# VectorE instead of TensorE turns the layer input, with the retention output and the second memory layer's norm rearranged

## The reference, cut to what matters

```python
def first_block(x, mem, ...):
    for i in range(2):
        if i % 2 == 0:
            tok, mq, z = retention_branch(x, positions, w_in_ret[j], ret_norm_g[j])
        else:
            tok, mq, z = gdn_branch(x, w_in_gdn[j], ...)
        mem_out = memory_attention(mq, mem, w_mem_kv[i])   # kv = mem @ w_kv
        branch = concat([tok, mem_out]) * silu(z)
        y = branch @ w_out[i]
        x = layer_norm(ALPHA * x + y, ln_g[i], ln_b[i])
    return x
# retention, at its end, per head:
    mu, var = mean(o, -1), mean(square(o - mu), -1)
    o = (o - mu) * rsqrt(var + NORM_EPS) * norm_g
```

## Time and profile before

| | us |
|---|---|
| median of 3 runs | 2926.92 |
| lowest, highest | 2924.23, 2928.47 |
| the profiled execution, its time | 2937.41 |
| its span | 2935.6 |
| TensorE matmuls busy | 2867.0 (98%) |
| GpSimd busy | 2344.0 (80%) |
| ScalarE busy | 1364.8 (46%) |
| VectorE busy | 1205.2 (41%) |

### The profile page before, as it was taken

How to read it: one execution, slowest core, us unless ns; L and a number is a source line. 1 busy time by engine, 2 the same in 40 slices (tenths; PEclk the granted TensorE clock), 3 DMA queues, 4 the chain that set the end, 5 groups by cost and what they waited for, 6 DMA issues and landing times.

```text
span 2935.6 us, 40528 instructions
## 1 busy us (share of the span) xinstructions
PE 2867.0 (98%) x13819; PEld 2406.5 (82%) x13819; DVE 1205.2 (41%) x2325; ACT 1364.8 (46%) x1783; POOL 2344.0 (80%) x1831
## 2 busy tenths in 40 slices
PE   9989999999979999999999999999999999999998
PEld 7878788888868888888888888788887888888886
DVE  5253343434442433334333345486535332332334
ACT  4444444444434554544546354555435444444444
POOL 8978898888877665757667588788887999999997
PEclk9999999999999999999999999999999999999999
DMA  8545555555654444434444356444554655655553
GB/s 285 190 161 182 165 191 190 180 188 178 209 180 135 144 143 134 147 122 154 140 138 145 117 172 203 157 140 153 196 164 163 200 194 188 200 186 192 197 193 132
DMA packets 284353, 502.72 MB, mean 171 GB/s; under 512 B 18021, under 2 KB 68662, under 8 KB 283190
## 3 DMA queue, kind: packets, MB, share of 16 engines
q1 hardware_dynamic: 275606, 482.55, 50.0%
q10 hardware_dynamic: 8608, 18.24, 1.7%
HBM read 498.61 MB, written 2.12 MB: 171 GB/s over the span
## 4 chain that ended last, share of the span: by engine, by line
POOL 51%; issue 25%; PE 23%; POOLq 1%; DVE 0%; DVEq 0%; ACT 0%
POOL wlo L418 51%; PE acc L474 8%; PE acc L475 8%; PE acc L476 8%; POOLq L416 0%; POOLq L413 0%; DVE x_sb L2316 0%; POOLq L418 0%; DVE big L2292 0%; DVE kv L1808 0%; DVEq L154 0%; ACT small L1427 0%; DVE small L2283 0%; POOL eps_sb L412 0%; DVE small L2309 0%
## 5 line engine op out<-in xcount | busy, mean ns | idle before, releaser
L418 POOL TENSOR_TENSOR wlo<-raw,whi 128x512 fp32r<-128x512 f32 x1824 | 2343.5, 1317 | 574.5 <-ACT whi L1050 558.2
L1050 ACT ACTIVATE whi<-raw 128x1024 fp32r<-128x1024 f32 x910 | 957.5, 1060 | 1102.6 <-PE acc L476 1058.1
L474 PE MATMUL acc<-whi,a_lo 128*128 128x512 f32 x2528 | 1002.9, 397 | 37.5 <-DVE kv L1773 19.4
L476 PE MATMUL acc<-whi,a_hi 128*128 128x512 f32 x2528 | 988.7, 391 | 0.0
L475 PE MATMUL acc<-wlo,a_hi 128*128 128x512 f32 x2528 | 987.6, 391 | 0.0
L474 PEld LDWEIGHTS acc<-whi,a_lo 128*128 128x128 f32 x2528 | 477.4, 189 | 135.7 <-DVE kv L1773 19.9
L476 PEld LDWEIGHTS acc<-whi,a_hi 128*128 128x128 f32 x2528 | 476.5, 189 | 101.0
L475 PEld LDWEIGHTS acc<-wlo,a_hi 128*128 128x128 f32 x2528 | 477.4, 189 | 95.5
L474 PE MATMUL acc<-whi,b_lo 128*128 128x512 f32 x928 | 365.6, 394 | 0.0
L476 PE MATMUL acc<-whi,b_hi 128*128 128x512 f32 x928 | 361.4, 389 | 0.0
L475 PE MATMUL acc<-wlo,b_hi 128*128 128x512 f32 x928 | 361.2, 389 | 0.0
(11 more groups left out here) (291 smaller groups left out, 2103.2 us busy)
## 6 DMA issues: line engine op xcount, KB each, us to landing
raw<-in_w_in_ret SPq DMA_DIRECT2D x176, 512.0 KB, 4.4
raw<-in_w_in_gdn SPq DMA_DIRECT2D x176, 512.0 KB, 4.3
raw<-in_w_out SPq DMA_DIRECT2D x160, 512.0 KB, 4.5
raw<-in_w_mlp_in SPq DMA_DIRECT2D x128, 512.0 KB, 4.3
raw<-in_w_mlp_out SPq DMA_DIRECT2D x128, 512.0 KB, 4.4
raw<-in_w_in SPq DMA_DIRECT2D x80, 512.0 KB, 4.6
raw<-in_w_mem_kv SPq DMA_DIRECT2D x63, 512.0 KB, 4.8
cb<-log_decays ACTq DMA_DIRECT2D x6, 512.0 KB, 5.6
```

The source lines that it names most:

```text
L418: part = pool.tensor_tensor(wlo[q % 4][:, c], raw_half[:, c], whi[q % 4][:, c].bitcast(f32), ALU.subtract)
L474: pe.matmul(dst, l, w_h, start=start and block == 0, stop=False)
L476: mm = pe.matmul(dst, h, w_h, start=False, stop=stop and block == KB - 1)
L1050: act.activation(whi[q % 4][:, :], raw[j][:, (q % 2) * HALF:(q % 2 + 1) * HALF], ACT.Copy).then_inc(hi_ready, 1)
```

## The change

`turn_x` is not called for `x0` and `x1` any more. VectorE gets `turn_chunk`: 16 block transposes (the last in two parts, 17 instructions) from x_sb into the two banks of a chunk, and the low parts of a chunk follow behind the turn of the next. In the retention output the subtraction and the inverse deviation are one operation in place in the bank, and one product per bank with z writes `br`. In the second memory layer ScalarE's root of the norm goes from behind unit 35 to behind the last chunk of the memory (beside unit 34), and VectorE turns the first keys behind three of the norm's four chunks. The diff, without the lines of plumbing (the callback arguments `last` and `x_between` on TensorE, `after` handed through `layer_norm`):

```diff
-            kv_units("kv1", U_KV1, W_KV1, 4 * B_L1, lambda q: turn_mem("mem1", 1, 3) if q == 1 else None, "mem1", 2,
-                     lambda c: turn_x("x1", x_sb, 1, c))
+            kv_units("kv1", U_KV1, W_KV1, 4 * B_L1, lambda q: turn_mem("mem1", 1, 3) if q == 1 else None, "mem1", 2)
...
             chunk_mem(3)
+            layer_norm(0)
             for q in range(5, 8):
                 half(U_KV1, q)
 
-            kv_slots(U_KV1, W_KV1, lambda: layer_norm(0), "x1", gates_loaded, gates_hi)
+            kv_slots(U_KV1, W_KV1, lambda: None, "x1", gates_loaded, gates_hi)
...
-            def by_chunks(chunk, part=None):
+            def by_chunks(chunk, part=None, after={}):
 
                 for c in range(4):
                     chunk(c)
+                    if c in after:
+                        after[c]()
...
+            def turn_chunk(phase, c):
+
+                (a, na), (b, nb) = (fill(phase, f"f{f}") for f in (2 * c, 2 * c + 1))
+                to = squares(banks[a // 2], "b t")
+                x = x_sb[:, :].rearrange("p (t c) -> p t c", t=TT)[:, :, c * COL:(c + 1) * COL].rearrange("p t (b c) -> p b t c", b=KB)
+                for bk, n in ((a, na), (b, nb)):
+                    if n > 1:
+                        dve.wait_ge(emptied[bk], n - 1)
+
+                def square(i, j, blocks):
+                    return dve.transpose(to[32 * j:32 * (j + 1), blocks, :, 32 * i:32 * (i + 1)], x[32 * i:32 * (i + 1), blocks, :, 32 * j:32 * (j + 1)])
+                for i in range(4):
+                    for j in range(4):
+                        if (i, j) != (3, 3):
+                            square(i, j, slice(0, KB))
+                square(3, 3, slice(0, 2)).then_inc(filled[a], 1)
+                square(3, 3, slice(2, 4)).then_inc(filled[b], 1)
...
             def ret_end(g, i):
                 dve.wait_ge(wide_taken, 2 * (W_RET + 3 * g + 3))
                 for h in range(2):
+                    b, _ = full("ret", f"o{h}", g)
+                    for t in range(TT):
+                        n, c = 2 * h + t, slice(t * SEQ, (t + 1) * SEQ)
+                        ts(b[:, c], b[:, c], small[:, 24 + 2 * n:25 + 2 * n], small[:, 40 + n:41 + n], SUB, MUL)
+                dve.drain()
+                for h in range(2):
                     b, done = full("ret", f"o{h}", g)
-                    for t in range(TT):
-                        n, c = 2 * h + t, slice(t * COL + h * SEQ, t * COL + (h + 1) * SEQ)
-                        last = stt(out=br[:, c], in0=b[:, t * SEQ:(t + 1) * SEQ], scalar=small[:, 24 + 2 * n:25 + 2 * n], in1=zs[:, c],
-                                   op0=SUB, op1=MUL)
-                    last.then_inc(done, 1)
-                dve.drain()
-                for h in range(2):
-                    for t in range(TT):
-                        n, c = 2 * h + t, slice(t * COL + h * SEQ, t * COL + (h + 1) * SEQ)
-                        last = ts(br[:, c], br[:, c], small[:, 40 + n:41 + n], None, MUL)
-                last.then_inc(s["branch_ready"], 1)
-                dve.drain()
+                    to = br.rearrange("p (t c) -> p t c", t=TT)[:, :, h * SEQ:(h + 1) * SEQ]
+                    z = zs.rearrange("p (t c) -> p t c", t=TT)[:, :, h * SEQ:(h + 1) * SEQ]
+                    tt(to, b[:, :].rearrange("p (t c) -> p t c", t=TT), z, MUL).then_inc(done, 1)
+                dve.drain().then_inc(s["branch_ready"], 1)
                 turn_out("ret", g, br)
...
-            a_parts("x0", 1)
+            dve.wait_ge(s["x_loaded"], 16)
+            for c in range(4):
+                turn_chunk("x0", c)
+                if c:
+                    a_part(2 * c - 2, "x0", 1)
+                    a_part(2 * c - 1, "x0", 1)
+            a_part(6, "x0", 1)
+            a_part(7, "x0", 1)
             scale_x()
             dve.drain()
...
-            layer_norm(0)
-            keys(U_KV1, W_KV1, 0)
+            layer_norm(0, None, {2: lambda: keys(U_KV1, W_KV1, 0)})
             keys(U_KV1, W_KV1, 1)
 
             n48 = 2 * NVH
-            for f in range(6):
-                a_part(f, "x1", 3)
+            for c in range(4):
+                turn_chunk("x1", c)
+                if c:
+                    a_part(2 * c - 2, "x1", 3)
+                    a_part(2 * c - 1, "x1", 3)
             dve.wait_ge(s["ab_hi"], 1)
```

More of the change, by code:

```diff
@@ L576, in branch, with kv_units @@
                 turn_natural(phase, ("ba", "bb"), g, br)
-            def kv_units(phase, m, w, added, first, mem, count, last):
+            def kv_units(phase, m, w, added, first, mem, count):
                 wide_of_new(m, 0, w, added - 1, first, mem, count)
@@ L583, in kv_units @@
                 wide(m + 2, 0, w + 1, added)
-                wide(m + 3, 1, w + 2, added, loads(last))
+                wide(m + 3, 1, w + 2, added)
             def ret_scores(g):
@@ L956, in _ @@
             first_between = turn_others(lambda c: turn_mem("mem0", 0, c), turn_columns)
[L958 to L963, removed]
+            kv_units("kv0", U_KV0, 0, 0, first_between, "mem0", 0)
             layer(U_RET, W_RET, 0, ret_steps, "ret", "att0", None, "x0", 1,
                   lambda q: turn_mem("mem1", 1, (q - 3) // 2) if q in (3, 5, 7) else None)
-            kv_units("kv1", U_KV1, W_KV1, 4 * B_L1, lambda q: turn_mem("mem1", 1, 3) if q == 1 else None, "mem1", 2,
-                     lambda c: turn_x("x1", x_sb, 1, c))
+            kv_units("kv1", U_KV1, W_KV1, 4 * B_L1, lambda q: turn_mem("mem1", 1, 3) if q == 1 else None, "mem1", 2)
             def gate_steps(q):
@@ L1879, in ret_end @@
                 for h in range(2):
-                    b, done = full("ret", f"o{h}", g)
+                    b, _ = full("ret", f"o{h}", g)
                     for t in range(TT):
-                        n, c = 2 * h + t, slice(t * COL + h * SEQ, t * COL + (h + 1) * SEQ)
-                        last = stt(out=br[:, c], in0=b[:, t * SEQ:(t + 1) * SEQ], scalar=small[:, 24 + 2 * n:25 + 2 * n], in1=zs[:, c],
-                                   op0=SUB, op1=MUL)
-                    last.then_inc(done, 1)
+                        n, c = 2 * h + t, slice(t * SEQ, (t + 1) * SEQ)
+                        ts(b[:, c], b[:, c], small[:, 24 + 2 * n:25 + 2 * n], small[:, 40 + n:41 + n], SUB, MUL)
                 dve.drain()
                 for h in range(2):
-                    for t in range(TT):
-                        n, c = 2 * h + t, slice(t * COL + h * SEQ, t * COL + (h + 1) * SEQ)
-                        last = ts(br[:, c], br[:, c], small[:, 40 + n:41 + n], None, MUL)
-                last.then_inc(s["branch_ready"], 1)
-                dve.drain()
+                    b, done = full("ret", f"o{h}", g)
+                    to = br.rearrange("p (t c) -> p t c", t=TT)[:, :, h * SEQ:(h + 1) * SEQ]
+                    z = zs.rearrange("p (t c) -> p t c", t=TT)[:, :, h * SEQ:(h + 1) * SEQ]
+                    tt(to, b[:, :].rearrange("p (t c) -> p t c", t=TT), z, MUL).then_inc(done, 1)
+                dve.drain().then_inc(s["branch_ready"], 1)
                 turn_out("ret", g, br)
@@ L2171, in layer, with layer_norm @@
                 dve.drain()
-            def layer_norm(i, part=None):
+            def layer_norm(i, part=None, after={}):
                 for t in range(TT):
@@ L2190, in chunk @@
                             op0=MUL, op1=ADD).then_inc(s["x_final"], 1)
-                by_chunks(chunk, part)
+                by_chunks(chunk, part, after)
             def scale_x():
```

## The result

| | before | after |
|---|---|---|
| median of the runs timed side by side, us | 2927.69 (2924.23 to 2930.03, 4 runs) | 2906.85 (2901.93 to 2910.93, 4 runs) |
| profiled execution: time, span, clock | 2937.4, 2935.6, 0.99 | 2904.5, 2902.7, 0.995 |

The ratio is 0.9929 [0.9909, 0.9949]: 20.8 us faster, at 2906.85. Forecast were 34.9 us and 2892, with a range up to 2904. The two profiled executions differ by 32.9.

A forecast was written before the change was run, and what follows sets the result against it. TensorE was taken to set the pace, with GpSimd close behind. The terms -19.8 - 21.1 + 2.4 + 1.9 + 1.7 = -34.9 us, taken off the median 2926.92, gave 2892 us, range 2879 to 2904.

The forecast's parts named there:

- the retention output's term: Multiplications of br moved into the bank end TensorE's stalls in two groups, 11.4 and 8.35 us: -19.8 us.
- the sentence that carries the whole sum from the profiled execution to the median: The sum, made against an execution 10.5 us above the median, was taken off the median 2926.92 unchanged.
- Second memory layer: Earlier root and keys turned before unit 36 end TensorE's stall, -21.1 us; new short waits cost +2.4.
- The root: ScalarE's root in the second memory layer's norm, 28.02 us late before, would come near 826, norm starting about 826.6.
- the lockstep: VectorE's norm in the second memory layer alternates with GpSimd's pieces, 1.65 us each; three chunks take 19.8 us.
- the short waits: TensorE's waits from the norm's slowing of GpSimd in the second memory layer: +2.4 us, bounds 0 and 4.7.
- Turns of x: Turning x0 and x1 on VectorE saves TensorE 3.5 us a layer but adds waits and slow clock: +1.9 and +1.7.
- Both waits: TensorE waits 3.7 us at half 3 of unit 4 and 3.5 us in front of the gates.
- A: Rival: turns of x are hidden and nothing new waits; -47.9 us, 2879 us; chance 0.15.
- B: Rival: scale_x is shut out by GpSimd, first layer costs +8.4; sum -28.4, 2898 us; chance 0.25.
- C: Rival: new tensor_scalar waits like the old, or ScalarE's wait has another cause; -15.1, 2912 us; chance 0.07.
- D: Rival: each of 136 transposes out of x_sb waits for a GpSimd piece; about +95, 3022 us; chance 0.03.

The follow-up runs named there:

- experiment 1: The kernel before, run again with no edit; 2929.48 us, ratio 0.9999.
- experiment 2: The kernel before with only the retention output's new form; 2921.51 us, ratio 0.997 to the kernel before.
- experiment 7: The changed kernel with scale_x behind group 0's rotation and ScalarE's parts of the last chunk behind its work for half 3; 2896.65 us, ratio 0.99.
- experiment 5: The changed kernel run again, unchanged; 2906.76 us, ratio 0.9923 to the kernel before.
- experiment 9: The kernel before with the last of the four operations ahead of the retention output's multiplications issued once more; 2924.36 us.
- experiment 4: The kernel before with the new retention output and the rearranged second memory layer, x still turned by TensorE; 2902.86 us, ratio 0.9909.

## Why the forecast was wrong

**The step that failed** is the retention output's term, -19.8 us, together with the sentence that carries the whole sum from the profiled execution to the median. The term is 11.4 for group 0 and 8.35 for group 1. Group 1's is there in every trace of the old form; 8.1 measured for the part. Group 0's was there in the execution that I read and, by their times, in one of the 41 runs of the kernel before in the first two batches (30, and 11 of experiment 1). That execution was 10.5 us above the median, and the three runs of before spread over 4.2: the text names the 10.5 and then passes over it. With -8.1 the sum is -23.2, 2903.7 us, inside the range, against 2906.85 measured. Against an execution with the stall the pair of profiles has 32.9, near the 34.9. So the waits and their places were right and the size of one term wrong. One sentence behind the term holds for group 0 of that trace and not in general: a tensor_scalar that meets GpSimd's series was kept out until GpSimd paused in two of six traces at group 0; in the other four, and in all six at group 1, it was let in while the series went on.

**Second memory layer**, -21.1 + 2.4 = -18.7: -17.5 measured alone. The root, the lockstep of 1.65 us a piece (1.70 in the trace after), and the keys before unit 36 came as worked out; the short waits are 1.4 us, inside the bounds.

**Turns of x**, +3.6: +3.9 to +5.9 against the run without them, by the two ways of comparing, and +6.1 [2.9, 10.3] on the kernel before. So this term was put low, if anything; with -26.7 for the two parts and +6.1 the sum is -20.6, against the 20.8 measured. Both waits were within 0.4 us of their forecast, at the places named. What I took as the price of turning x0 was the price of its place in ScalarE's queue.

**The rivals.** A fell with those two waits. B fell: scale_x took 3.01 us. It came at 0.43 into a series, where the one shut out came 14 into it. C fell in experiment 2: without the old form no group stalls. D fell: 7.58 us a chunk. How long a tensor_scalar in SBUF is kept out is not one figure: at group 0 the first of the four took 0.74 to 1.30 us in the four traces in which it was let in behind piece 12, and 12.70 and 13.82 in the other two; at group 1 it took 8.15 to 9.29. The products of bank and zs were not kept out: all twelve last 0.68 to 0.69 us, those beside a GpSimd that never paused too, against a mean of 0.69 before.

**The best version** is experiment 7: 2896.65 and 2897.37 us, 31.9 below the kernel before in the second batch, 10.1 below the changed kernel. In it VectorE turns both inputs, and neither scale_x nor the last chunk's high parts stand ahead of work that is due.

## What to carry to other kernels

Before a stall of a trace goes into a sum, ask whether the traced execution is a usual one: where it lies above the median by as much as one of its stalls, price the change with that stall and without it. When work moves to an idle engine, look for what is queued behind its result on a third engine; moving that back in the queue, with scale_x, was worth more here (6.1 us at its place) than the move itself (4.0). Keep tensor_scalar between two SBUF tiles out of a stretch in which GpSimd works without a pause, or do it in a bank: in the first two groups four of them took 5.20 to 14.61 us in SBUF in the kernel before's two traces, and group 0's four in the bank 1.91.

## What the hardware showed that I had not expected

A multiplication that meets a long series of GpSimd's pieces isn't always let in after the piece that it came in. In six traces it ended at few places: 15.27 us (four times) or 27.76 to 27.77 us (twice) into a series of 22 pieces, and 30.25 to 30.27 us into one of 26, whether it came at 20.98 or at 22.10. That is some 0.15 us behind the ends of pieces 12, 22 and 24. Once one is let in while the series goes on, the three behind it follow a piece apart (5.20 us for four). In the later groups, where GpSimd mostly pauses 0.17 us after every second piece, four took 1.1 to 5.3 us. Why piece 12 was missed in one execution and taken in another at the same arrival, and why it is piece 24 in group 1, stays open.

The clock's slow stretches are a second source of scatter. After the same wait of 2.37 us the same 16 matmuls took 2.06 us in one execution, at a granted clock of 0.94 (experiment 7), and 3.67 in another, at 0.50 (experiment 5). The changed kernel's two traces, with spans of 2902.7 and 2905.7, have one such group and two. Between 940 and 2880 the granted clock is below full in 3 windows of 20 us in the one and in 6 in the other, in 3 of experiment 1 (span 2927.8), 0.83 to 0.95 in each of these, and in none of experiment 9 (2922.5) or experiment 4. So these two executions of one kernel differ by 3.0 us with next to no difference in who waits for whom: none of TensorE's waits differs between them by over 0.5 us in sum.
